# Gate, xbc and z projections of an encoder step as three products of split operands, on one core

## The reference

```python
hp = rmsnorm(yp, norm_mix_g[l])
proj = h @ w_in
a_val, a_gate, z, xbc, dt_raw = jnp.split(
    proj, [CONF_DIM, 2 * CONF_DIM, 2 * CONF_DIM + SSD_DIM, 2 * CONF_DIM + SSD_DIM + SSD_XBC], axis=-1)
a_glu = a_val * jax.nn.sigmoid(a_gate)
a_conv, new_conf_state = causal_dwconv(a_glu, conf_state, conf_w, conf_b)
a_out = jax.nn.silu(layernorm(a_conv, ln_g, ln_b))
xbc_c, new_xbc_state = causal_dwconv(xbc, ssd_conv_state, xbc_w, xbc_b)
xbc_c = jax.nn.silu(xbc_c)
```

## Time and profile before

| | us |
|---|---|
| median of 3 runs (lowest, highest) | 1737.77 (1737.29, 1738.06) |
| span of the profiled execution | 1735.7 |
| PE busy | 1702.0 |
| DVE busy | 1058.7 |
| ACT busy | 683.9 |
| POOL busy | 370.5 |

### The profile page before, as it was taken

One profiled execution on the slowest core, in us unless ns is written; L12 is line 12 of the kernel. 1 busy time (PEld: TensorE's weight loads), 2 busy tenths in 40 slices (PEclk: granted clock), 3 DMA queues, 4 the chain that ended last, 5 costly groups with the idle time before them and its releaser, 6 DMA issues.

```text
span 1735.7 us, 27688 instructions
## 1 busy us (share of the span) xinstructions
PE 1702.0 (98%) x11360; PEld 1543.0 (89%) x11360; DVE 1058.7 (61%) x1717; ACT 683.9 (39%) x1219; POOL 370.5 (21%) x289
## 2 busy tenths in 40 slices
PE   7999998999999999999999999999999999999999
PEld 6566556797999999999989899789899999999999
DVE  3699867637667647465654424744676774655574
ACT  4111243435525525253552124633543453544352
POOL 3012100211104324132213132200110241414240
PEclk9999999999999999999999999999999999999999
DMA  8222330142303131403143221603320313122212
GB/s 263 101 77 103 93 107 28 49 195 98 104 27 138 32 130 46 135 19 128 31 141 74 75 73 64 246 27 114 153 93 25 128 48 115 61 70 86 87 66 91
DMA packets 39674, 162.30 MB, mean 94 GB/s; under 512 B 9384, under 2 KB 10280, under 8 KB 25600
## 3 DMA queue, kind: packets, MB, share of 16 engines
q1 hardware_dynamic: 32240, 124.59, 21.5%
q0 software_dynamic: 7312, 35.98, 5.8%
HBM read 149.87 MB, written 10.42 MB: 92 GB/s over the span
## 4 chain that ended last, share of the span: by engine, by line
PE 92%; DVE 5%; ACT 2%; issue 1%; DMA 0%; POOL 0%; SPq 0%; DVEq 0%; ACTq 0%
PE G L940 68%; PE S L940 11%; PE Q L940 11%; PE Q L1635 1%; ACT work L1731 0%; DVE rstd L2344 0%; DMA ring<-in_w_mk 0%; DVE ev_low L2593 0%; ACT rstd L1731 0%; DVE stats L2623 0%; DVE resid L2875 0%; ACT h_split L1731 0%; PE Q L1347 0%; DVE stats L2992 0%; DVE work L2636 0%
## 5 line engine op out<-in xcount | busy, mean ns | idle before, releaser
L940 PE MATMUL G<-ffn_rows,w_split 128*128 128x320 f32 x2160 | 329.8, 309 | 0.0
L940 PEld LDWEIGHTS G<-ffn_rows,w_split 128*128 128x128 f32 x2160 | 320.1, 188 | 0.0
L1731 ACT ACTIVATE w_split<-ring 128x512 fp32r<-128x512 f32 (+2 forms) x224 | 159.1, 711 | 316.8 <-PE G L940 208.4
L940 PE MATMUL G<-front,ring 128*128 128x128 f32 (+2 forms) x832 | 223.3, 430 | 11.0 <-DMA ring<-in_w_mk 9.3
L940 PEld LDWEIGHTS G<-front,ring 128*128 128x128 f32 x832 | 133.0, 193 | 100.0 <-issue 95.9
L856 POOL TENSOR_TENSOR mkT<-ring 128x512 f32<-128x512 f32 x72 | 98.2, 1369 | 564.6 <-DMA ring<-in_w_up 382.2
L940 PE MATMUL G<-h_split,w_split 128*128 128x320 f32 x1344 | 200.9, 310 | 1.2 <-DVE w_split L2359 0.8
L940 PEld LDWEIGHTS G<-h_split,w_split 128*128 128x128 f32 x1344 | 197.5, 188 | 1.9 <-issue 1.3
L940 PE MATMUL G<-g_split,w_split 128*128 128x320 f32 x1056 | 163.7, 310 | 0.1
L940 PEld LDWEIGHTS G<-g_split,w_split 128*128 128x128 f32 x1056 | 156.7, 188 | 1.7 <-DVE w_split L2848 1.4
L2715 DVE TENSOR_TENSOR w_split<-ring,w_split 128x512 fp32r<-128x512 f32 (+1 forms) x124 | 105.8, 854 | 59.9 <-ACT w_split L1731 58.7
(11 more groups left out here) (351 smaller groups left out, 2818.8 us busy)
## 6 DMA issues: line engine op xcount, KB each, us to landing
ring<-in_w_up SPq DMA_DIRECT2D x44, 1024.0 KB, 4.8
ring<-in_w_down SPq DMA_DIRECT2D x48, 256.0 KB, 2.6
ring<-in_w_down SPq DMA_DIRECT2D x32, 320.0 KB, 2.9
front<-in_mem_k POOLq DMA_DIRECT2D x8, 1024.0 KB, 6.1
front<-in_mem_v POOLq DMA_DIRECT2D x8, 1024.0 KB, 10.6
ring<-in_w_mk SPq DMA_DIRECT2D x4, 1024.0 KB, 5.9
ring<-in_w_mv SPq DMA_DIRECT2D x4, 1024.0 KB, 10.9
ring<-in_w_glu SPq DMA_DIRECT2D x4, 1024.0 KB, 8.6
```

Of the source, the lines that this page charges most:

```text
L940: return nc.tensor.matmul(out, lhsT, rhs, start=start, stop=stop, **kw)
L1731: return nc.scalar.activation(*a, **k)
```

## The change

Nineteen of the twenty tiles of glu, xbc and z (all but glu 0) are computed from split rows and split weights. The rows' high part x_hi is written over x, whose contents are read from memory a second time before the output projection is added; the low part h_lo is written over h, block by block, as tile 0 (`front_plain`) has used the block. ACT makes x_hi and the weights' high parts (`front_high_part`, two instructions of 128x512 a tile), POOL the weights' low parts (`front_low`, two of 128x512), in place in the ring, and DVE the rows' low part. The high weights lie in room that z's gates and the scan use later. `narrow` now runs over x_hi and h_lo. Both convolutions are as before: their running sums stay in SBUF.

```diff
+            def front_low(n):
+                pool.wait_ge(front_high, n)
+                src, lo = front_piece(n)
+                for half, hi in enumerate(front_hi(n)):
+                    ks = slice(4 * half, 4 * half + 4)
+                    ins = nc.gpsimd.tensor_tensor(lo[:, ks], src[:, ks], hi.bitcast(F32), ALU.subtract)
+                ins.then_inc(front_split, 1)
+
             memory_keys(0)
+            for n in range(1, 3):
+                front_low(n)
             pool.wait_ge(pads_in, 16 * 12)
             for j in range(4):
+                if j in (1, 2):
+                    front_low(2 * j + 2)
+                if j < 3:
+                    front_low(2 * j + 3)
                 read_wait(pool, TILE0["glu"] + 2 * j + 1)
...
             memory_keys(1)
+            for n in range(8, 10):
+                front_low(n)
             for j in range(KD):
+                front_low(10 + j)
...
+            for n in range(18, 20):
+                front_low(n)
...
+            def front_project(n, halfway=None):
+                begin(front_tile(n))
+                out = GF[front_tile(n) % 2]
+                pe.wait_ge(front_split, n)
+                hi, lo = front_hi(n), front_piece(n)[1]
+                for k in range(KD):
+                    if n == 1:
+                        pe.wait_ge(mix_low, k + 1)
+                    for part, (w, xs) in enumerate(((hi[k // 4][:, k % 4, :], x_hi), (hi[k // 4][:, k % 4, :], h_lo),
+                                                    (lo[:, k, :], x_hi))):
+                        for f in range(2):
+                            fr = slice(f * HT, (f + 1) * HT)
+                            m = mm(out[:, fr], w, xs[:, k, fr], k + part == 0, k == KD - 1 and part == 2)
...
             memory_keys(0)
             memory_values(0)
-            projections("glu", 8, KD, rows(h), norm="mix0")
-            narrow(TILE0["dtp"], "wdt", h)
+            front_plain()
+            for n in range(1, 8):
+                front_project(n)
+            narrow(TILE0["dtp"], "wdt", x_hi[:, :, :].bitcast(F32), h_lo[:, :, :].bitcast(F32))
...
+            def front_high_part(n):
+                c = front_chunk(n)
+                act.wait_ge(chunk_in[c % RING], 16 * (c // RING + 1))
+                if n >= 3:
+                    tile_wait(act, front_tile(n - 2))
+                for half, hi in enumerate(front_hi(n)):
+                    ins = A(hi, front_piece(n)[0][:, 4 * half:4 * half + 4], ACT.Copy)
+                ins.then_inc(front_high, 1)
...
+            for k in range(KD):
+                act.wait_ge(applied, APPLIED["mix0"] - KD + 1 + k)
+                A(x_hi[:, k, :], h[:, k, :], ACT.Copy).then_inc(mix_high, 1)
+            front_high_part(2)
...
-            for j in range(6):
+            for j in range(4):
                 xbc_rows(j)
-            for j in range(2):
-                xbc_silu(j)
+                front_high_part(10 + j)
+            xbc_silu(0)
+            xbc_rows(4)
+            front_high_part(14)
+            xbc_silu(1)
+            xbc_rows(5)
+            front_high_part(15)
...
             xbc_silu(2)
             xbc_rows(6)
+            front_high_part(16)
             act.wait_ge(applied, APPLIED["mean"])
             for k in range(4):
                 square(acc[:, k, :])
+            xbc_rows(7)
+            front_high_part(17)
             xbc_silu(3)
-            xbc_rows(7)
             z_gate(0)
+            front_high_part(18)
             xbc_silu(4)
...
+            for k in range(KD):
+                if k < KD - 1:
+                    dve.wait_ge(mix_used, k + 1)
+                else:
+                    tile_wait(dve, TILE0["glu"])
+                dve.wait_ge(mix_high, k + 1)
+                v.tensor_tensor(h_lo[:, k, :], h[:, k, :], x_hi[:, k, :].bitcast(F32), ALU.subtract).then_inc(mix_low, 1)
...
+                if c == CHUNK["q0"]:
+                    tile_wait(sp, z_tile(3))
+                    for k in range(0, KD, 2):
+                        sp.dma_start(x[:, k:k + 2, :], dram["x"][:, k:k + 2, :]).then_inc(x_in[k // 2], 16)
```

More of the change, by code:

```diff
@@ L265, in pr @@
             return par[0:rows, o:o + 1]
+        with nc.sbuf_tensor("resid_split", [P, KD, T], F32R) as x_hi:
+            pass
         x = sb("resid", [P, KD, T])
@@ L467, in fv_piece, with front_tile, front_chunk, front_piece @@
             return src, fv_hi[:, half, i // 2 * 256:(i // 2 + 1) * 256], fv_low(i // 2)[:, half]
+        def front_tile(n):
+            return TILE0["glu"] + n if n < 8 else xbc_tile(n - 8) if n < 16 else z_tile(n - 16)
+        def front_chunk(n):
+            name, i = ("glu", n) if n < 8 else ("xbc", n - 8) if n < 16 else ("z", n - 16)
+            return CHUNK[name] + i // 2
+        def front_piece(n):
+            src, lo = (w[:, front_chunk(n) % RING, :].rearrange("p (k n) -> p k n", k=KD)[:, :, n % 2 * P:(n % 2 + 1) * P]
+                       for w in (ring, ring_r))
+            return src, lo
+        ZS_AT, HT_AT = KD * T + scan_room, xbcc_at + KD * T + 8 * T
+        def front_hi(n):
+            places = {18: (HT_AT, HT_AT + 512), 19: (ZS_AT + 2048, HT_AT + 1024)}
+            ats = places.get(n, (ZS_AT + n % 2 * 1024, ZS_AT + n % 2 * 1024 + 512))
+            return [front_r[:, at:at + 512].rearrange("p (k n) -> p k n", k=4) for at in ats]
         def evout_piece(i):
@@ L1036, in residual_stat, with narrow @@
                 stat(1, 2, ones, width)
-            def narrow(n, wname, rows_of):
+            def narrow(n, wname, *parts):
                 out = begin(n)
                 pe.wait_ge(par_in if wname == "wdt" else wf_ready, 16 if wname == "wdt" else 1)
[L1042 to L1046, removed]
+                for part, rows_of in enumerate(parts):
+                    for k in range(KD):
+                        q, o = k % 4, PAR[wname][0] + k * NH
+                        rows, w = slice(32 * q, 32 * q + 32), par[:, o:o + 32]
+                        ends = part == 0 and k < 4, part == len(parts) - 1 and k >= 4
+                        mm(out[rows, 0:512], w, rows_of[:, k, 0:512], *ends, tile_position=(0, 32 * q))
+                        m = mm(out[rows, 512:T], w, rows_of[:, k, 512:T], *ends, tile_position=(0, 32 * q))
                 m.then_inc(tile_done, 1)
@@ L1120, in _ @@
             memory_values(1)
[L1121 to L1125, removed]
+            for n in range(8, 18):
+                front_project(n)
+                if n == 13:
+                    conv_stat(3)
             nready[0] += 4
@@ L1138, in _ @@
                 .then_inc(tile_done, 1)
-            s = chunk(CHUNK["z"] + 1)
-            for n in range(2, 4):
-                project(z_tile(n), s, n % 2 * P, KD, rows(h), halfway=h_free if n == 3 else None)
+            front_project(18)
+            front_project(19, halfway=h_free)
             RUN, CSK = NCH - 1, 64 + NH
@@ L1857, in memory_values @@
                 A(mv[:, 0, m2, :], G[n % 2][:, 0:512], ACT.Copy, scale=mem_rtok[:, m2:m2 + 1]).then_inc(read[n % 2], 1)
[L1859 to L1862, removed]
             for j in range(4):
@@ L1884, in _ @@
                     read_wait(act, t0 + 2 * (j - 2) + 1)
-                evacuate(tmp[:, j % 2, :], t0 + 2 * j, ACT.Sigmoid)
+                evacuate(tmp[:, j % 2, :], t0 + 2 * j, ACT.Sigmoid, out=GF)
+                if j in (1, 2):
+                    front_high_part(2 * j + 2)
+                if j < 3:
+                    front_high_part(2 * j + 3)
             act.wait_ge(par_in, 16)
@@ L1895, in xbc_rows @@
                 a, b = padded(xbcp, j, XW - 1, XPROMPT, XREQ, XW - 1)
-                A(a, G[n % 2][:, 0:SEQ], ACT.Copy)
-                A(b, runs(G[n % 2][:, SEQ:T]), ACT.Copy).then_inc(read[n % 2], 1)
+                A(a, GF[n % 2][:, 0:SEQ], ACT.Copy)
+                A(b, runs(GF[n % 2][:, SEQ:T]), ACT.Copy).then_inc(read[n % 2], 1)
             def xbc_silu(j):
@@ L1904, in z_gate @@
             def z_gate(j):
-                evacuate(zs[:, j, :], z_tile(j), ACT.Silu)
+                evacuate(zs[:, j, :], z_tile(j), ACT.Silu, out=GF)
             act.wait_ge(dt_abs, 1)
@@ L2905, in _ @@
             n = TILE0["evout"]
+            for i in range(KD // 2):
+                dve.wait_ge(x_in[i], 32)
             dve.wait_ge(ev_used, 1)
```

29 lines of the change are left out of this document (25 added, 4 removed).

## The result

The change made the kernel slower: 1769.26 us (1769.05 to 1769.44, four runs) against 1737.59 (1737.29 to 1738.06, four runs), a ratio of 1.0182 with a 95% interval of 1.0167 to 1.0196. The forecast was 1757.3, and 1769.26 lies 0.26 above the range.

The account below looks back on a forecast made before the run. PE and DVE were taken as almost level, with POOL's low parts holding up DVE. Scan start 16.8 us later plus 2.7 clock loss gave 19.5; 1735.7 + 19.5 + 2.1 = 1757.3 us, range 1744 to 1769.

Parts of the forecast that it names:

- Step 1 (PE): Split tiles take 7.11 us against 8.67 on PE, the step-size product 2.40 us more: net 27.2 us less.
- step 5: Chain over DVE, PE, ACT and POOL up to the scan: it begins at 276.5 against 259.7, 16.8 us later.
- Steps 2, 3 and 7: ACT's copies (about 0.7 us per weight copy), DVE's low-row subtractions and the second reading of x (9.5 us) are hidden.
- step 3: DVE's eight low-row subtractions after the norm, about 0.75 us each, hidden by 1.2 us; if not, 1 to 2 us.
- Step 4: POOL's low weights beside DVE: each costs DVE 2.25 us, 17 cost 38.3 us; POOL's own stretches from 2.4 to 2.9.
- The 16 us before the mean's sum: In the chain, PE waits 16 us for the first running sums, which end at 213.2.
- The wait behind ACT's first SiLU: ACT's SiLU precedes evacuation of xbc tile 4, so tile 14 starts at 222.3, 8 us behind the mean's sum.
- Step 6: PE's clock after standing still 8.5 us before tile 17: 2.7 us lost, between 0 and twice that.
- Of "right": Signs: scan near 277, low parts 1.3 to 1.5 us, single slow taps, DVE 45 us busier, PE waits, 7.1 us tiles.
- the three waits of PE: Signs of right: PE waits about 16 us for the first sums, near 8 before xbc tile 6 and z tile 1.
- Of "wrong": Signs: taps keeping 0.466 us on average, no PE wait over 5 us before 250, or a wait on x's second reading.
- late low parts: Rival: POOL's pieces each wait some 2.7 us longer, tiles 14, 15, 17 start later: 1762 to 1768 us, chance 0.13.

Follow-up runs that it names:

- the run with three drains: Changed kernel, with DVE waiting for its own last tap at three places among the 108 taps behind the step sizes: 1753.47 us, ratio 1.0087.
- the run with drains after every 8th tap: Changed kernel, with DVE waiting for its own last tap after every eighth tap of the first convolution, no instruction added: 1760.33 us.

## Why the prediction was wrong

The sign and the engine pair were right, the place where the price is paid was not. By its steps:

- *Step 1 (PE)* was right. `narrow` takes 2.40 and 2.41 us, a split tile 7.04, and the memory keys begin at 120.61, where step 5 had 121.7 + 0.9 = 122.6 for the last multiply.
- *Steps 2, 3 and 7* were right: h_lo and ACT's copies are hidden, the first multiply starts at 63.56 (63.5 predicted), and the second reading of x lands in 8.7 us unseen. One thing in step 3 was already the coming loss in small: tile 2's subtraction waited for the end of the row of h_lo subtractions on DVE, 5.14 us instead of 1.28. No tile needed it sooner.
- *Step 4 failed.* It took "almost its whole length" for what a low part costs DVE, and "POOL's own stretches from 2.4 to 2.9" for all that it costs POOL, from rows 6 where the two engines took turns. The first half holds where POOL gets in: 2.24 us in the run with three drains. The second does not: subtractions took 9.99, 21.45 and 28.99 us, each until the end of a row of taps, and PE waited up to 38.35 us for them. DVE had its sums done at 202.2 and not 213.2: it lost 13.8 us instead of 24.75. Of the 11.0 us between, 6.75 are three of the eleven low parts that had not been made by then.
- *What the trace before had shown.* A product of POOL behind taps, 3.46 us, went to a rival with 0.13, at 2.7 us apiece. Nothing bounded that wait by 2.7. The row of 28 taps beside it ends at 118.18 + 13.04 = 131.22, and the product, about 0.8 us when nothing holds it, ends at 131.80: it had waited for the end of the row, and that could have been read. Rows 6 has only four DVE instructions, and the change puts POOL beside rows of up to 60 taps.
- *The rule that step 4 cites* ("SBUF — State Buffer" in the Trainium skill, section "Who interferes with whom") names the pair rightly. By its other half neither a VectorE instruction with one SBUF input nor a GpSimd instruction that only writes SBUF is in a collision. With that agree the taps with their sum in PSUM (2.54 us a pair of subtractions), POOL's memsets (0.525 us) and the gate multiply at 81.12, which took 0.68 us as before beside the subtraction that it let in. A block's first two instructions, with one SBUF input each, did lose time when POOL got in (1.84 instead of 0.78 us). The rule excepts some modes of VectorE, and no run here shows whether they ran in one. The same page of the Trainium skill, in the section "SBUF: two separate sides", has the one that starts first keep the shared ports for its whole instruction, so that the loser waits for one. Here it waited for up to 60 taps in the changed kernel, and for more in the run with small memsets.
- *Step 5.* The 16 us before the mean's sum did not occur, since PE was 38 us late for it. In the run with drains after every 8th tap, where POOL takes its turn, they were 15.8. The wait behind ACT's first SiLU did not occur either, and was 7.6 us with the sums in PSUM. The chain was worked out for a kernel that needs step 4 to hold.
- *Step 6* had the right size for one wait and the wrong number of them. Tile 9 starts at 198.11 and tile 10 at 207.53: 9.42 us against 7.04. Tile 4 has 8.48 and tile 17 has 9.14, so 5.9 us in all, where the forecast had 2.7 once. The slower pace is the lower level of the clock: from 198 to 203 us the granted clock reads 0.50, so 1.2 GHz, and two matmuls come every 0.53 us; from 203 to 208 it reads 0.98, and they come every 0.29. PE had done nothing for 38.35 us before.
- *The signs named.* Of "right", three came: low parts of 1.3 to 1.5 us (the median), single taps a microsecond longer, split tiles at 7.1. The scan at 277, DVE busier by 45 us (31.5 measured) and the three waits of PE did not, but for 5.55 us before z tile 1. Of "wrong", none came as worded: the taps kept their 0.464 us over the long rows, but over all 240 they took 121.0 us instead of 113.6, so 0.50 each instead of 0.47. No sign named the thing to look for, a long instruction on POOL.
- *The range.* The rival "late low parts" was right in kind and priced at 1762 to 1768. Its price should have had the length of a row of taps as its upper end.

Shown by the runs is that the collision between POOL's reading of SBUF and taps whose running sum lies in SBUF makes the loss (sums in PSUM, POOL writing only, and the kernel before with its sums in PSUM as the control), that POOL can be kept out for as long as DVE's row of taps goes on, and that a wait of DVE for its own last tap let it in at the three places where it stood waiting at one (one with drains after every 8th tap, two with three drains), as before the mean's sum in the changed kernel. Open is what lets POOL in without a drain, and what a drain does that idle time before a memset does not. The moment of arrival within a pair of taps does not decide it. In the six kernels with POOL's subtractions and the sums in SBUF, the first subtraction of 22 low parts arrived up to 0.45 us after the start of a 512-wide tap: 13 were let in at the next tap, 9 were not. Of nine that came 0.46 to 0.65 us after it, one was.

## What to carry to other kernels

An engine with a busy share of 21% is not free if its instructions read SBUF beside VectorE instructions that read two tensors there. Look for what the neighbour runs without a break, and price the wait by the length of that run, not by one instruction. Where a long chain of two-operand VectorE instructions stands beside GpSimd work that reads SBUF, keep the running operand in PSUM (41.6 us here). If there is no room, give the work to VectorE itself (25.4 us), or let VectorE wait for its own last instruction at a few places (15.8 us for three such waits). In a trace, look for few instructions with much busy time: a mean far above the median is a wait that the profile counts as work. And where one instruction in a trace took unusually long, look at what its end coincides with: that says how long the next one can get.

## What was not expected of the hardware

- A GpSimd subtraction of 128x512 with SBUF operands, 1.28 us alone, was held until it had taken 21.45, 28.99, 32.51 and once 50.6 us beside VectorE taps of 0.464 us each. Rows of 46 and 60 taps took as long as without it (21.35 and 27.82 us).
- A memset on VectorE between them, of 128x1 or of 128x512 into PSUM (0.48 us, with 0.11 us of idle time before it), did not end this; a wait of VectorE for its own last tap did, with idle time of only 0.04 us at two places and 0.21 us at a third.
- The low parts are cheaper on the full engine than on the nearly idle one: 1743.85 against 1769.26 us. VectorE makes one in 1.27 us, and loses 2.24 us where GpSimd makes it.
